# A seven-product block scheme for the gate and up products of the second feed-forward stage

## What is computed

```python
def rms_norm(x, g):
    y = xf * lax.rsqrt(jnp.mean(xf * xf, axis=-1, keepdims=True) + NORM_EPS)
    return (y * g.astype(jnp.float32)).astype(x.dtype)

def swiglu(x, w_in, w_out):
    gate, up = jnp.split(x @ w_in, 2, axis=-1)
    return (jax.nn.silu(gate) * up) @ w_out

def encoder_layer(x, lp):
    x = x + 0.5 * swiglu(rms_norm(x, lp['norm_ffn1']), lp['ffn1_w_in'], lp['ffn1_w_out'])
    ...
    x = x + mixed @ lp['w_out']
    x = x + 0.5 * swiglu(rms_norm(x, lp['norm_ffn2']), lp['ffn2_w_in'], lp['ffn2_w_out'])
    return x
```

## Time and profile before

| | us |
|---|---|
| median of 3 runs | 3520.48 |
| lowest, highest | 3517.74, 3520.85 |
| span of the profiled execution | 3518.2 |
| PE busy in it | 3407.2 (97%) |
| PEld busy | 3216.6 (91%) |
| DVE busy | 1794.4 (51%) |
| ACT busy | 980.4 (28%) |
| POOL busy | 50.4 (1%) |

### The profile page before, as it was taken

The page is one execution under the profiler, slowest core; times in us unless marked ns, Lnnn a source line. Parts: engine busy times, 40 slices in busy tenths (PEclk is TensorE's granted clock), DMA queues, the critical chain, the costliest instruction groups (busy, mean ns, idle before and its releaser), DMA issues.

```text
span 3518.2 us, 60866 instructions
## 1 busy us (share of the span) xinstructions
PE 3407.2 (97%) x26620; PEld 3216.6 (91%) x26620; DVE 1794.4 (51%) x3152; ACT 980.4 (28%) x1607; POOL 50.4 (1%) x62
## 2 busy tenths in 40 slices
PE   7999999999998999999999999999999979999998
PEld 7999999888776999999999999998877669999998
DVE  5443445664888443333454434456558774333334
ACT  4222223222454321221331212232234633212222
POOL 0000000000000000000000000000000000000000
PEclk9999999999999999999999999999999999999999
DMA  3222121331051212112122221132310511222121
GB/s 137 59 74 74 61 66 61 107 105 63 4 195 53 90 53 80 58 60 73 56 75 78 68 77 54 66 104 73 105 43 21 211 60 61 61 71 62 53 72 63
DMA packets 78457, 264.30 MB, mean 75 GB/s; under 512 B 8739, under 2 KB 8739, under 8 KB 76913
## 3 DMA queue, kind: packets, MB, share of 16 engines
q1 hardware_dynamic: 74640, 248.08, 21.3%
q0 software_dynamic: 3552, 12.34, 1.1%
HBM read 230.50 MB, written 29.88 MB: 74 GB/s over the span
## 4 chain that ended last, share of the span: by engine, by line
PE 91%; DVE 6%; issue 1%; ACT 1%; DMA 1%; SPq 0%; DVEq 0%; ACTq 0%
PE ps L782 90%; DVE uv L2272 1%; DVE rstd L1816 0%; PE ps L1315 0%; DMA x<-xT 0%; DVE sc L2322 0%; DMA gtab<-hyc 0%; DVE M2X L2045 0%; ACT mh L1744 0%; DVE Mrk L2032 0%; DVE hout L2423 0%; DVE ktok L2033 0%; DVE olocal L2171 0%; DVE mixed L2243 0%; DVE kap L2079 0%
## 5 line engine op out<-in xcount | busy, mean ns | idle before, releaser
L782 PE MATMUL ps<-hh,wh 128*128 128x384 f32 (+2 forms) x3520 | 1188.7, 338 | 11.6 <-DVE hl L1824 10.6
L782 PE MATMUL ps<-hl,wh 128*128 128x384 f32 (+2 forms) x3520 | 1179.8, 335 | 0.0
L782 PE MATMUL ps<-hh,wl 128*128 128x384 f32 (+2 forms) x3520 | 1179.4, 335 | 0.0
L782 PEld LDWEIGHTS ps<-hh,wh 128*128 128x128 f32 x3520 | 663.6, 189 | 35.2 <-issue 16.3
L782 PEld LDWEIGHTS ps<-hl,wh 128*128 128x128 f32 x3520 | 663.9, 189 | 15.3 <-issue 0.3
L782 PEld LDWEIGHTS ps<-hh,wl 128*128 128x128 f32 x3520 | 663.5, 188 | 14.2
L1450 ACT CAST wh<-wring 128x1024 fp32r<-128x1024 f32 (+2 forms) x372 | 346.1, 955 | 660.7 <-PE ps L782 655.3
L782 PE MATMUL ps<-act_high,wl 128*128 128x384 f32 x1408 | 470.3, 334 | 0.0
L782 PE MATMUL ps<-act_high,wh 128*128 128x384 f32 x1408 | 470.3, 334 | 0.0
L782 PE MATMUL ps<-act_low,wh 128*128 128x384 f32 x1408 | 470.3, 334 | 0.0
L1930 DVE TENSOR_TENSOR silu<-ps,rstd 128x384 f32<-128x384 f32 x176 | 98.0, 557 | 700.7 <-PE ps L782 700.5
(11 more groups left out here) (266 smaller groups left out, 3318.3 us busy)
## 6 DMA issues: line engine op xcount, KB each, us to landing
wring<-wa SPq DMA_DIRECT2D x244, 512.0 KB, 3.6
wring<-wa SPq DMA_DIRECT2D x64, 384.0 KB, 3.1
wring<-wa SPq DMA_DIRECT2D x64, 320.0 KB, 3.0
bias<-bias SPq DMA_DIRECT2D x24, 512.0 KB, 7.3
conv_q_k<-stage SPq DMA_DIRECT2D x28, 384.0 KB, 2.6
kern_rows<-kst POOLq DMA_DIRECT2D x12, 512.0 KB, 3.2
outT<-x SPq DMA_DIRECT2D x2, 3072.0 KB, 10.2
kern<-kern_rows SPq DMA_DIRECT2D x12, 512.0 KB, 7.3
```

The lines of the kernel that those rows point to most:

```text
L782: return pe.matmul(out, lhsT, rhs, start=start, stop=stop)
```

## The change

Only the second stage of each layer changes. Take one hidden tile j. Its gate weights are two halves by features, G1 and G2 (512 each), its up weights U1 and U2. The normed input is four blocks, features by tokens: X11 (features 1, tokens 1), X12, X21, X22. Gate and up for both token halves are a 2x2 by 2x2 block product, eight block products before. The change forms seven:

| unit | weights | input | bank |
|---|---|---|---|
| 0 | G1 | X11 | 0 |
| 1 | U1+U2 | X12-X11 | 2 |
| 2 | U1+U2-G1 | T = X22-X12+X11 | onto 0 |
| 3 | G2 | X21 | 1 |
| 4 | G1-U1 | X22-X12 | onto 0 |
| 5 | G2+G1-U1-U2 | X22 | onto 2 |
| 6 | U2 | X21-T | onto 0 |

Each unit is 4 feature tiles by three matmuls, 12 matmuls of 128x384; banks are 3 higher for odd j. A partial result that is also needed by itself is copied out of its bank by ACT before the next unit goes onto it (`hold`, after units 0, 1, 2) and added back by DVE at the end (`first_gate`, `second_up`, `second_gate`). The weight sums are made by four GpSimd instructions of 128x512 per hidden tile, three of them in one buffer. ACT and DVE split seven half tiles of 128x512 in place of two tiles of 128x1024. The input sums are made once, in `mix_out`, by `pair_first` and `pair_second` in place of `x_done`; `mix_out` therefore does its output tiles in the order 0, 4, 1, 5, 2, 6, 3, 7. The stage has five blocks (5, 5, 4, 4, 4 tiles) in place of four (6, 6, 5, 5), since the buffers of activations shrink. A gate tile leaves the ring `wring` when unit 4 has been split, an up tile when unit 6 has.

```diff
-FF_BLOCKS = [(0, 6), (6, 6), (12, 5), (17, 5)]
+FF_BLOCKS = [[(0, 6), (6, 6), (12, 5), (17, 5)], [(0, 5), (5, 5), (10, 4), (14, 4), (18, 4)]]
...
+M_ORDER = (0, 4, 1, 5, 2, 6, 3, 7)
...
+        SUM_AT = {1: 0, 2: 0, 4: 1, 5: 0}
+        SUM_DONE = {1: 1, 4: 2, 2: 3, 5: 4}
...
+        def released(n):
...
+                return s_ulo, UNITS * (FT * l + j) + (7 if side else 5)
...
+            def weight_sums(l, j):
...
+                pool.tensor_tensor(wsum[:, 0, :, :], u1, u2, ALU.add).then_inc(s_wsum, 1)
+                pool.tensor_tensor(wsum[:, 1, :, :], g1, u1, ALU.subtract).then_inc(s_wsum, 1)
+                pool.wait_ge(s_ulo, UNITS * J + 2)
+                pool.tensor_tensor(wsum[:, 0, :, :], wsum[:, 0, :, :], g1, ALU.subtract).then_inc(s_wsum, 1)
+                pool.wait_ge(s_wsum, 4 * J + 3)
+                pool.wait_ge(s_ulo, UNITS * J + 3)
+                pool.tensor_tensor(wsum[:, 0, :, :], g2, wsum[:, 0, :, :], ALU.subtract).then_inc(s_wsum, 1)
...
+                        product(l, j, 0)
...
+                        product(l, j, 1)
+                        pe.wait_ge(s_held, 3 * J + 1)
+                        product(l, j, 2)
+                        product(l, j, 3)
+                        if j == 0:
+                            norm()
+                        pe.wait_ge(s_held, 3 * J + 3)
+                        product(l, j, 4)
+                        product(l, j, 5)
+                        pe.wait_ge(s_exit, 4 * J + 2)
+                        product(l, j, 6)
...
+            def pair_second(l, i):
...
+                STT(t2[:, a2, :], x[:, KH + i, HALF:T], gain, t1[:, a1, :], M, SU).then_inc(s_t, 1)
+                ve.wait_ge(s_t, 4 * g0 + 2)
+                TT(t3[:, a3, :], t2[:, a2, :], y1[:, :], SU).then_inc(s_t, 1)
+                STT(t4[:, a4, :], x[:, KH + i, 0:HALF], gain, t2[:, a2, :], M, SU).then_inc(s_t, 1)
```

More of the change, by code:

```diff
@@ L772, in _ @@
                 m.then_inc(s_clear, 1)
+                for j in range(FT):
+                    weight_sums(l, j)
         @block.tensor
@@ L916, in ffn, with mm3_onto @@
                                 m = mm3(bank(4 + v % 4, HALF), w_k(w, k), (ah[:, k, cols], al_[:, k, cols]),
+                                        k == 0, k == nj - 1)
+                            m.then_inc(s_fo, 1)
+            def mm3_onto(out, lhs, rhs, start, stop, onto):
+                for n, (a, b) in enumerate(((0, 0), (0, 1), (1, 0))):
+                    m = pe.matmul(out, lhs[a], rhs[b], start=start and n == 0, stop=stop and n == 2, skip_group_check=onto)
+                return m
@@ new lines, in ffn_pairs, with ahead @@
+            def ffn_pairs(l):
+                n = use_base(l, 3)
+                after = "norm_ffn1" if l + 1 < LAYERS else None
+                for b, (j0, nj) in enumerate(FF_BLOCKS[1]):
+                    n += 2 * nj
+                    split[0] = n
+                    last = b == len(FF_BLOCKS[1]) - 1
+                    cap = LAYERS * USES - 1 if last else n + OUT_TILES - 1
+                    def ahead(j, i):
+                        if j + 1 < j0 + nj:
+                            unit_low(l, j + 1, i)
+                        elif i in (2, 4, 6):
+                            split_to(n + i // 2 - 1)
+                    for j in range(j0, j0 + nj):
+                        if j > j0:
+                            first_up(l, j - 1)
+                            gate_up(l, j - 1, 0)
+                        ahead(j, 0)
+                        if j > j0:
+                            act_low1(l, j - 1, 1)
+                            act_low1(l, j - 1, 0)
+                        ahead(j, 1)
+                        ahead(j, 2)
+                        ahead(j, 3)
+                        if j == 0:
+                            norm()
+                        first_gate(l, j)
+                        ahead(j, 4)
+                        second_up(l, j)
+                        ahead(j, 5)
+                        second_gate(l, j)
+                        ahead(j, 6)
+                        gate_up(l, j, 1)
+                    first_up(l, j)
+                    gate_up(l, j, 0)
+                    act_low1(l, j, 1)
+                    act_low1(l, j, 0)
+                    for m in range(OUT_TILES):
+                        split_to(min(n + 2, cap))
+                        n += 1
+                        if not last and m == 7:
+                            for i in (4, 5):
+                                unit_low(l, j + 1, i)
+                        for v in range(2):
+                            add_out(l, 1, 16 * b + 2 * m + v, 0.5, 4)
+                        if last and m == 0 and after:
@@ L1952, in zero_pads, with pair_done @@
+            def pair_done(l, p):
+                (pair_second if p % 2 else pair_first)(l, p // 2)
             def zero_pads(bufs):
```

510 lines of the change are left out of this document (409 added, 101 removed).

## The result

The changed kernel takes **3475.04 us** (median of 4 runs, 3473.38 to 3477.81) against 3520.66 for the kernel before (4 runs, 3517.74 to 3521.13): ratio **0.9872, 95% interval 0.9858 to 0.9886**. 3480 was predicted, with a range of 3452 to 3512. The profiled run is the longest of the four, with a span of 3476.0 us.

What follows compares the result with a forecast made beforehand. The prediction took TensorE's number of matmuls in the second stage as the bound. 3518.2 - 91.5 + 22.1 + 18 + 10.6 = 3477.4 us span, with 2.3 for the median 3479.7, so 3480; range 3452 to 3512.

Steps and rivals of the forecast that it cites:

- The matmuls: Second stage, both layers: 84 matmuls a hidden tile in place of 96, 528 fewer at 0.1733 us, 91.5 us saved.
- The mid-block loss: Hidden tiles inside a block: period 15.2 us against TensorE's 14.56, 0.65 a tile over 34 tiles, 22 us lost.
- the walk: Step-by-step count of one hidden tile's work on DVE, GpSimd and ACT, giving 15.2 us where TensorE needs 14.56.
- The sharing: DVE instructions with both inputs in SBUF and GpSimd's sums hold each other up; four sums, 5.1 us, largely DVE time too.
- rival (a): Middle of a block: sums fit into DVE's waits, TensorE stays the bound, period 14.56, time 3458; chance 0.21.
- The start: Start of the second stage: TensorE stalls ahead of units 0, 1, 4, 6 and in the next tile; 9 us a layer.
- the extra 0.8 in the next tile: Start of the stage: one more TensorE stall of 0.8 us, in the hidden tile after the first.
- The blocks: Block ends and starts: stalls into output tiles 2.3 us a layer, with those out of them 5.3 a layer, 10.6 in all.
- The sum: Whole kernel: 3518.2 less 91.5 plus 22.1, 18 and 10.6 gives a span of 3477.4 us, a median of 3480.
- third rival: Second stage: GpSimd's sums are slower than their shown 1.28 us and pace the stage; period over 16.4; chance 0.10.
- (c): GpSimd paces the stage: a sum of 1.59 us, period 16.4, cancels the gain; at 1.75, 3543 us; chance 0.10.

Runs made afterwards that it cites:

- copy-first kernel: Changed kernel with ACT's third copy out of PSUM (`hold`) put ahead of the cast of unit 2; 3458.69 us, ratio 0.9823.
- the short fills: Changed kernel with each GpSimd sum replaced by four constant fills that read nothing, all waits kept; 3448.69 us, ratio 0.9799.
- the new order at the start: Kernel with sums on VectorE, plus start-of-stage splits and casts of units 4 and 5 moved later, ACT's first copy ahead of two casts; 3450.38 us.

## Why the prediction was right, point by point

**The matmuls, -91.5.** Holds: without sums or with them on VectorE the period is 14.56, the number of matmuls (84) times 0.1733.

**The mid-block loss, 22 us.** Right in mechanism, too large in size. The period is 15.10 where I had 15.2, and TensorE waits where I said, ahead of units 4 and 6, for the third copy and `second_up`. The pause is 0.53 a tile, not 0.65. And not all 17 tiles of a layer pay: all such pauses of layer 0 add up to 6.9 us, 13 times 0.53, and those of layer 1 to some 6.5, since some start with weights in hand (block 2 pays in one tile and a half out of four; that this is why is argued, not tested). About 13.5 us, not 22. In the last tile of a block I expected the gate result after 14.56; it came after 13.01, since VectorE has nothing to prepare there and takes it earlier, and no term rests on it. What the walk did not see is that its loop goes through the transfer: I had the up tile landed 0.4 before it was needed, and it is the transfer that releases the first sum [the first line of the middle of a block]. So part of the agreement between 15.2 and 15.10 is luck.

**The sharing.** I wrote that the fourth sum holds back the split of unit 3. It does, by a lead of 0.06 us. That makes it the least certain line of the walk, and the most expensive one: with the other order the loop is under 14.56 and rival (a) comes true, as in the copy-first kernel at 3458.69, where (a) said 3458 (the equal number is partly chance, as that kernel gains at the block starts too). The prediction should have priced the two orders. It gave (a) 0.21 for another reason, the sums fitting in beside waits.

**The start, 9 us a layer.** The size came out (9.2 to 9.8 in layer 0), its pieces did not, so here the number is in part luck. Unit 0 paused 2.00 (2.6 predicted), unit 6 1.39 (2.6). Unit 1 paused 1.68 and 2.78 in place of 1.0: the walk of the start did not let the first two sums of tile 1 hold `pair_second`, the very thing that it counts in the middle of a block. The wait for a copy, 1.8 ahead of unit 4 in the prediction, was 1.60 ahead of unit 2, for the first copy, which stands behind two casts; the extra 0.8 in the next tile did not come. Unpredicted was the clock. The granted clock of the kernel after around the start, then that with the sums on VectorE:

```profile
1218.00:1232.00 14.00, 10.77 (x41) 9.81 (x42) 11.06 (x15) 8.04 (x14) 4.99 (x4) 0.76 0.17 59
```

```profile
1218.00:1232.00 14.00, 10.73 (x55) 9.54 (x56) 10.37 (x19) 9.88 (x16) 0.00 (x0) 1.00 0.15 39
```

At 0.76 TensorE was at the lower of its two levels, 1.2 GHz, for part of the stretch: behind the pause of 2.00 seven matmuls come 0.32 apart in place of 0.173, behind that of 1.60 ten more. The first seven stand ahead of a wait for VectorE's features and are hidden by it; the ten cost 1.5 us at most, which are in the 9.2 to 9.8.

**The blocks, 5.3 a layer.** Ends 0.45 plus 0.11 for a block of 4 (0.6 predicted), 0.09 for a block of 5 (0.25). Block 2 starts with 0.86 (0.85), but not for the reason given: the last `add_out` does not stand behind the splits of units 4 and 5, since VectorE sits idle 0.43 before it until TensorE's last output product is done [the line at 1342.38], and the pause is 0.86 in every kernel with the new scheme, with sums and without. The pause is the 0.2 to VectorE, the addition of 0.56 and 0.1 back; that the number agrees is luck. The two later starts with 1.33 and 0.96, each plus 0.11 (1.05 each) in layer 0, 0.68 and 0.65 in layer 1. Together 5.3 in layer 0.

**The sum.** In the stages the new scheme lost 21.9 us in layer 0 and 20.5 in layer 1, against 25.3 predicted for each: 8 us too much in all, nearly all in the mid-block term. The profiled run gave 7 back outside the stages (49.1 gained in them, 42.2 in the span): 1.9 ahead of the first, 0.7 behind the second, and 4.3 between them, where it took 1190.9 us from the last matmul on an activation tile of layer 0 to the first of layer 1's stage against 1186.7 before. Over the experiments, whose mixers are the same, that stretch is 1187.1 to 1191.0, so up to 4 us of it are spread between kernels and executions. The span, 3476.0 against 3477.4 predicted, is closer than its terms, and it is that of the longest of the four runs; by the medians, 3475.04 against 3480, the prediction is 5 us off.

**The page on the trace.** The third rival leaned on doubt about GpSimd's spans. Its sums stand back to back now: L874 starts at 1256.55, L875 at 1257.95, 1.40 apart, with a span of 1.44, and in all 44 such pairs the distance is 0.03 to 0.05 less than the span. The span could be trusted here, which the trace decides against that section of "Perfetto Trace Analysis" in the Trainium skill, for this instruction. The sums were 1.27 to 1.88, the medians of the four between 1.29 and 1.60, and the period 15.1, so (c) was far away.

## What to carry to other kernels

When work is given to a helper engine, count what it saves the busy one, not what the helper does: here 117.5 us of GpSimd a stage spared VectorE 17, and the same sums on VectorE made the kernel 26 us faster. Where two engines meet in a loop, price both orders in which they can meet; a lead of 0.06 us decided 1.1 us of the loop, and with it whether the loop or TensorE sets the period. And before moving work ahead at a start, ask whether its order or its amount is the bound: the reorderings of the start moved the pauses and took away 1 us a stage at most.

## What the runs showed of the hardware

- Where a VectorE instruction has both inputs in SBUF and a GpSimd instruction reads SBUF, the two take turns by who comes first, and whoever comes second waits for the whole instruction of the other: 1.78 for a split of 0.69 issued 0.06 after a sum of 1.30, 0.68 for one that was first, and then the sum takes 1.62. A VectorE instruction that reads PSUM is not held (0.56 beside a sum of 1.62). The Trainium skill, "SBUF — State Buffer", section "SBUF: two separate sides", calls this an exclusive lock that whoever starts first keeps for the whole instruction; the trace agrees, with these numbers.
- GpSimd's fills, which read nothing, do not hold VectorE: splits stay at 0.69 beside 1.3 us of them.
- TensorE's granted clock fell to a mean of 0.76 over 14 us after a stop of 2.00 us. With stops of 1.45, 0.78 and 1.60 in the same place it stayed at 1.00, and with 1.11, 0.78 and 1.60 (the short fills) it was 0.91 from 1214 to 1232. The length of a stop does not settle it alone: with the new order at the start, a stop of 2.00 kept full clock in layer 1 (1.00 from 2910 to 2945), and layer 0 with nearly the same stops had 0.88 from 1206.6 to 1236. What does settle it stays open.
